# First feed-forward layer of a three-block network: two pairs of column blocks in seven products behind five plain blocks, and the attention's mask added in the down part

## The chip, the cores and the metric

The kernel runs on one core of a Trainium2 chip. The metric is the device time of one execution in microseconds (us). TensorE (PE in the profile, PEld for its weight loads) multiplies, VectorE (DVE) and ScalarE (ACT) work elementwise, GpSimd (POOL) does small work and issues some transfers, SyncE (SP) issues the weight transfers.

## The reference, cut to what matters

The network has 256 tokens of width 1024 and runs a macaron block (feed-forward, attention and pooling mixer, feed-forward, gated projection) and then two more blocks with gated linear attention and retention, each between feed-forward layers. There are six feed-forward layers, all of this form, with an inner width of 2816:

```python
def swiglu(x, w_gate, w_up, w_down):
    return (jax.nn.silu(x @ w_gate) * (x @ w_up)) @ w_down

f = swiglu(rms_norm(h, ffn1_pre_g[i]), ffn1_w_gate[i], ffn1_w_up[i], ffn1_w_down[i])
h = h + 0.5 * rms_norm(f, ffn1_post_g[i])
```

The change touches the first of them, and the bias of the attention that comes behind it (`s = s + bias`, where keys outside a window of 16 columns are left out; the kernel does this with a mask of -1e30 that it adds to the bias).

## The kernel before

All is fp32, and each matmul is done in three: a weight block w is split into a high part (fp32r, made by ScalarE, L1436, tile `split`) and the rest (VectorE, L1876), the tokens likewise (`xh`, `xl`), and PE adds xh·high, xl·high and xh·rest. A weight block holds 4 x 128 rows and 512 columns (1 MB) and is loaded into a tile `whole`; `split` and `whole` are fourteen buffers that a plan hands out (`give_blocks`, by age), and a load or a split waits until PE has passed the block that was last in its buffer.

The gate and up part of a feed-forward layer has eleven column blocks j = 0 to 10 of 256 gate and 256 up columns. A *plain* block is two tiles, ("tile", j, 0) and ("tile", j, 1), one for each half of the 1024 input rows, and each tile is multiplied with both halves of the 256 tokens: 2 x 12 matmuls of 128 x 512. A *pair* of blocks (j, j+1) can instead be done in *seven products* of 12 matmuls each, in the manner of Strassen and Winograd: `b11`, `t1`, `t2`, `b22`, `t3`, `b21`, `t4`. The weights of b11, b22 and b21 are loaded as they are. Those of t1 and t3 are differences of two blocks that stand in memory: SP loads one, and a transfer that GpSimd issues adds the other to it (`pool_sum`, L650; called an addend below). Those of t2 and t4 are sums that VectorE makes (`dve_sum`, L1880). The token side has sums too (`sx`, split into `sh`, `sl`: "token sums" and "blocks"). b11, t2, t3 and t4 gather in PSUM bank 6, t1 with b22 and b21 in bank 7, and the results pass through u1, s5, u2 (ScalarE copies) and the combinations c12, c22, c11 (VectorE, L2157, L2163, L2169). Of the last, c4, there is no copy: ScalarE's gate (L1569) and VectorE's multiplication (L2143) read bank 6 itself.

After a block's silu and multiplication it is transposed by PE (("turn", j), four transposes, L783), split by ScalarE (`th`, L1441) and VectorE (`tl`, L1923), and is the token side of the down part.

What runs when is written out by hand: a list of steps (`LATE_PAIR` for the first layer `f1`, `TWO_PAIRS` for the other five) is walked by PE, ScalarE and VectorE each, and every engine does its part of each step in that order. The splits are run ahead by a few blocks (`ahead`, `behind`, from which buffers are free); in a product step VectorE does its combination, then the splits that are due (`lows()`), then its multiplication. PE's waits in a product are:

```python
def product(g, m):
    if m == "b11":
        if g:
            pe.wait_ge(vec.sem, vec.of("mult", name, grp[g - 1].first, 1))
        pe_product(pe, grp[g].b11, *x_block(0, 0), bank[6], True)
```

so the first product of a second pair waits until VectorE has made the last multiplication of the first pair from bank 6. `turn(7)` of a pair (7, 8) waits in the same way for the multiplication of that pair's c4.

GpSimd walks a list of its own (`pool_program`): two gains and the mask are loaded, then sixteen transfers bring the attention's bias (`pool_bias`), each behind a wait for one of VectorE's splits, with the two addends of f1 among them, and from the ninth on with the additions of the mask (`pool_mask`, L668, sixteen of them) between.

## Time and profile before

| | |
|---|---|
| time, median of 3 runs | 1591.44 us (1590.81 to 1591.67) |
| the profiled execution's own time | 1591.92 us |
| its span | 1590.1 us |
| PE busy | 1580.2 us (99%), 7659 matmuls |
| DVE busy | 1118.8 us (70%) |
| ACT busy | 866.0 us (54%) |
| POOL busy | 105.0 us (7%) |
| gate and up part of f1 on PE, up to the first matmul of the down part | about 6.7 to 132.3 us |

The profile gives for each engine how long it was busy, for a stretch the instructions in order of time (merged where alike), and for an engine what ended its idle time. Starts are from the span's start. The span is 1.8 us shorter than the execution's own time. A matmul of 128 x 512 is listed with 0.39 us and the next one starts 0.227 us after it, since they are pipelined; so PE's progress is read from starts. The same holds in small for DVE and ACT: an operation's listed time is some 0.08 or 0.1 us more than the distance to the next one's start.

### The profile page before, as it was taken

Reading aid. Unit: us, or ns where it says so; the run is one execution under the profiler, and the core shown is the slowest. Engines: PE = TensorE matmul, PEld = TensorE weight load, DVE = VectorE, ACT = ScalarE, POOL = GpSimd, SP = SyncE. Lnnn points to the kernel's source line nnn. Section 1 sums busy time; section 2 is a strip of 40 time slices with the busy share of each in tenths; the row PEclk is TensorE's granted clock in tenths of the full one; section 3 lists DMA queues with packets and bytes.
Section 4 is the critical chain, followed back from the end, with each engine's and each line's share of the span. In section 5 each row is a group of like instructions: output and inputs, shape, how many; then the busy total and the mean of one; then the engine's idle time right before and its main releaser. Section 6 shows DMA issues by size and latency. Waiting matters only on the chain.

```text
span 1590.1 us, 18691 instructions
## 1 busy us (share of the span) xinstructions
PE 1580.2 (99%) x7659; PEld 1317.9 (83%) x7659; DVE 1118.8 (70%) x1081; ACT 866.0 (54%) x907; POOL 105.0 (7%) x126
## 2 busy tenths in 40 slices
PE   9999999999999999999999999999999999999998
PEld 6888897788888888888988888888888998888886
DVE  6785566677875678865668886678856657688964
ACT  7564457556653766642655665366543435456650
POOL 0141000000000000001010000000000131000000
PEclk9999999999999999999999999999999999999999
DMA  8874463467854687562648765578545544587750
GB/s 339 247 237 190 179 245 133 159 252 231 282 181 172 263 280 265 177 240 96 238 159 310 232 225 213 224 229 287 211 185 196 192 172 152 189 292 233 242 212 27
DMA packets 51892, 341.38 MB, mean 215 GB/s; under 512 B 6240, under 2 KB 6624, under 8 KB 13408
## 3 DMA queue, kind: packets, MB, share of 16 engines
q1 hardware_dynamic: 44000, 301.94, 50.7%
q0 software_dynamic: 7584, 38.12, 10.8%
q8 instruction: 61, 1.00, 0.3%
q14 instruction: 23, 0.19, 0.0%
q10 hardware_dynamic: 224, 0.14, 0.0%
HBM read 339.12 MB, written 1.05 MB: 214 GB/s over the span
## 4 chain that ended last, share of the span: by engine, by line
PE 96%; DVE 2%; DMA 1%; ACT 1%; issue 0%; SPq 0%; DVEq 0%; ACTq 0%
PE bank L833 24%; PE bank L846 24%; PE bank L837 21%; PE bank L895 4%; PE bank L897 4%; PE bank L900 4%; PE bank L783 3%; PE bank L850 3%; PE bank L932 1%; PE bank L931 1%; PE bank L929 1%; DVE split L1876 1%; DMA h<-in_x 0%; DMA whole<-in_w_gla 0%; PE bank L1318 0%; PE bank L1108 0%
## 5 line engine op out<-in xcount | busy, mean ns | idle before, releaser
L1876 DVE TENSOR_TENSOR split<-whole,split 128x2048 fp32r<-128x2048 f32 (+2 forms) x329 | 704.4, 2161 | 203.8 <-ACT split L1436 202.1
L1436 ACT ACTIVATE split<-whole 128x2048 fp32r<-128x2048 f32 (+1 forms) x313 | 581.7, 1876 | 265.2 <-DVE whole L1880 38.7
L833 PE MATMUL bank<-split,xh 128*128 128x512 f32 x1052 | 288.1, 396 | 0.0
L846 PE MATMUL bank<-split,xh 128*128 128x512 f32 x1052 | 282.1, 390 | 0.0
L837 PE MATMUL bank<-split,xl 128*128 128x512 f32 x880 | 235.8, 390 | 0.0
L846 PEld LDWEIGHTS bank<-split,xh 128*128 128x128 f32 x1052 | 197.2, 188 | 41.8 <-DVE split L1876 0.4
L833 PEld LDWEIGHTS bank<-split,xh 128*128 128x128 f32 x1052 | 192.9, 188 | 40.7 <-issue 2.8
L837 PEld LDWEIGHTS bank<-split,xl 128*128 128x128 f32 x880 | 165.2, 188 | 35.4
L833 PE MATMUL bank<-split,th 128*128 128x512 f32 x524 | 143.7, 392 | 0.0
L837 PE MATMUL bank<-split,tl 128*128 128x512 f32 x524 | 142.2, 389 | 0.0
L846 PE MATMUL bank<-split,th 128*128 128x512 f32 x524 | 142.1, 389 | 0.0
L837 PEld LDWEIGHTS bank<-split,tl 128*128 128x128 f32 x524 | 98.4, 188 | 20.7
L846 PEld LDWEIGHTS bank<-split,th 128*128 128x128 f32 x524 | 98.4, 188 | 20.6
L833 PEld LDWEIGHTS bank<-split,th 128*128 128x128 f32 x524 | 97.1, 188 | 19.2
L929 PE MATMUL bank<-xh,split 128*128 128x256 f32 x256 | 72.6, 284 | 0.0
L931 PE MATMUL bank<-xl,split 128*128 128x256 f32 x256 | 72.4, 283 | 0.0
L932 PE MATMUL bank<-xh,split 128*128 128x256 f32 x256 | 72.4, 283 | 0.0
L1441 ACT ACTIVATE th<-bank 128x512 fp32r<-128x512 f32 x66 | 39.3, 597 | 29.1 <-PE bank L783 28.1
L1923 DVE TENSOR_TENSOR tl<-bank,th 128x512 fp32r<-128x512 f32 x66 | 45.3, 688 | 13.5 <-ACT th L1441 13.1
L1880 DVE TENSOR_TENSOR whole<-whole 128x2048 f32<-128x2048 f32 x22 | 50.3, 2284 | 0.0
L929 PEld LDWEIGHTS bank<-xh,split 128*128 128x128 f32 x256 | 49.1, 192 | 0.4 <-issue 0.3
L931 PEld LDWEIGHTS bank<-xl,split 128*128 128x128 f32 x256 | 49.1, 192 | 0.0
(312 smaller groups left out, 1727.0 us busy)
## 6 DMA issues: line engine op xcount, KB each, us to landing
whole<-in_w_a_gate_up SPq DMA_DIRECT2D x48, 1024.0 KB, 7.4
whole<-in_w_b_gate_up SPq DMA_DIRECT2D x48, 1024.0 KB, 7.1
whole<-in_w_f_gate_up SPq DMA_DIRECT2D x45, 1024.0 KB, 7.1
whole<-in_w_ret SPq DMA_DIRECT2D x24, 1024.0 KB, 4.9
whole<-in_w_f_down SPq DMA_DIRECT2D x20, 1024.0 KB, 4.9
whole<-in_w_a_down SPq DMA_DIRECT2D x20, 1024.0 KB, 4.9
whole<-in_w_b_down SPq DMA_DIRECT2D x20, 1024.0 KB, 5.1
whole<-in_w_mix SPq DMA_DIRECT2D x16, 1024.0 KB, 4.9
```

Of the source, the lines that this page charges most:

```text
L833: pe.matmul(o[:, :], tokens(0, k), whi[:, k, :], start=start and k == 0, stop=False, skip_group_check=True)
L837: pe.matmul(o[:, :], tokens(1, k), whi[:, k, :], start=False, stop=False, skip_group_check=True)
L846: ins = pe.matmul(o[:, :], tokens(0, k), wlo[:, k, :], start=False, stop=end, skip_group_check=True)
L895: pe.matmul(o[:, :], xh_of(k), whi[:, k, :], start=start and k == 0, stop=False, skip_group_check=True)
L897: pe.matmul(o[:, :], xl_of(k), whi[:, k, :], start=False, stop=False, skip_group_check=True)
L900: ins = pe.matmul(o[:, :], xh_of(k), wlo[:, k, :], start=False, stop=k == 3, skip_group_check=True)
L929: pe.matmul(o, whi[:, k, cols], xh[:, k0 + k, :], start=start and k == 0 and c % 2 == 0, stop=False, skip_group_check=True)
L931: pe.matmul(o, whi[:, k, cols], xl[:, k0 + k, :], start=False, stop=False, skip_group_check=True)
L932: ins = pe.matmul(o, wlo[:, k, cols], xh[:, k0 + k, :], start=False, stop=end, skip_group_check=True)
L1436: act.activation(split[s][:, 0:n], whole[r][:, 0:n], ACT.Copy).then_inc(hi.mark(i), 1)
L1876: dve.tensor_tensor(split[r][:, c0:c1], whole[r][:, c0:c1], split[s][:, c0:c1].bitcast(F32), ALU.subtract).then_inc(lo.mark(*what), 1)
L1880: dve.tensor_tensor(whole[load_to[i]][:, :], whole[load_to[a]][:, :], whole[load_to[b]][:, :], ALU.add).then_inc(vec.mark("sum", i), 1)
```

## The change

`LATE_PAIRS` takes the place of `LATE_PAIR`: blocks 5 and 6, which were plain, become a pair of seven products too. The order is blocks 0 to 3, tile (4, 0), the first product of pair (5, 6), tile (4, 1), and then the 14 products with the plain blocks 9 and 10 among them. GpSimd gets two more addends, and all sixteen bias transfers come first; the mask is added behind them, each two additions behind a split of one of the first blocks of the down part.

```diff
-LATE_PAIR = (
+LATE_PAIRS = (
...
-    ("tile", 4, 0), ("tile", 4, 1), ("turn", 3),
-    ("product", 0, "b11"), ("tile", 5, 0),
-    ("product", 0, "t1"), ("tile", 5, 1), ("turn", 4),
-    ("product", 0, "t2"), ("tile", 6, 0),
-    ("product", 0, "b22"), ("tile", 6, 1), ("turn", 5),
-    ("product", 0, "t3"), ("tile", 9, 0), ("turn", 6),
-    ("product", 0, "b21"), ("tile", 9, 1), ("turn", 8),
-    ("product", 0, "t4"), ("tile", 10, 0), ("tile", 10, 1), ("turn", 9), ("turn", 7))
+    ("tile", 4, 0), ("turn", 3),
+    ("product", 0, "b11"), ("tile", 4, 1),
+    ("product", 0, "t1"), ("product", 0, "t2"), ("tile", 9, 0), ("turn", 4),
+    ("product", 0, "b22"), ("product", 0, "t3"), ("tile", 9, 1),
+    ("product", 0, "b21"), ("product", 0, "t4"), ("turn", 6),
+    ("product", 1, "b11"), ("turn", 5), ("tile", 10, 0),
+    ("product", 1, "t1"), ("product", 1, "t2"), ("tile", 10, 1),
+    ("product", 1, "b22"), ("product", 1, "t3"), ("turn", 9),
+    ("product", 1, "b21"), ("product", 1, "t4"), ("turn", 8), ("turn", 7))
...
-LATE, TWO = Order(LATE_PAIR, 7), Order(TWO_PAIRS, 3, 7)
+LATE, TWO = Order(LATE_PAIRS, 5, 7), Order(TWO_PAIRS, 3, 7)
...
             for n in range(8):
-                if n == 2:
+                if n == 1:
                     pool_sum(pool, "t1", group["f1", 0].t1)
-                if n == 7:
+                if n == 5:
                     pool_sum(pool, "t3", group["f1", 0].t3)
                 pool.wait_ge(lo.sem, lo.of(6 + n))
                 pool_bias(0, n)
             for n in range(8):
+                if n == 3:
+                    pool_sum(pool, "t1", group["f1", 1].t1)
+                if n == 7:
+                    pool_sum(pool, "t3", group["f1", 1].t3)
                 pool.wait_ge(lo.sem, lo.of(14 + n))
                 pool_bias(1, n)
-                if n == 0:
-                    pool.wait_ge(bias_in[0].sem, bias_in[0].of(7))
-                pool_mask(0, n)
-            for hd in range(8):
-                pool.wait_ge(lo.sem, lo.of(22 + hd))
-                if hd == 0:
-                    pool.wait_ge(bias_in[1].sem, bias_in[1].of(7))
-                pool_mask(1, hd)
+            for t in range(2):
+                pool.wait_ge(bias_in[t].sem, bias_in[t].of(7))
+                for hd in range(8):
+                    pool.wait_ge(lo.sem, lo.of(at["f1d"][t] + hd // 2))
+                    pool_mask(t, hd)
```

The first place, PE, where the last product of a pair (t4, into bank 6) ends. Before, in the order of the program: t4 of the only pair, then block 10 in banks 0 and 1 (the first of its two tiles is shown).

```order
L783 MATMUL bank5<-ident,xn 128x128 x4
L895 MATMUL bank6<-split2,xh 128x512 x4
L897 MATMUL bank6<-split2,xl 128x512 x4
L900 MATMUL bank6<-split0,xh 128x512 x4
L833 MATMUL bank0<-split6,xh 128x512 x4
L837 MATMUL bank0<-split6,xl 128x512 x4
L846 MATMUL bank0<-split9,xh 128x512 x4
```

After, the last product of the first pair, one turn, and the first product of the second pair, again into bank 6 (lines stand two lower, L895 is L897):

```order
L897 MATMUL bank6<-split6,xh 128x512 x4
L899 MATMUL bank6<-split6,xl 128x512 x4
L902 MATMUL bank6<-split0,xh 128x512 x4
L785 MATMUL bank5<-ident,xn 128x128 x4
L897 MATMUL bank6<-split2,xh 128x512 x4
L899 MATMUL bank6<-split2,xl 128x512 x4
L902 MATMUL bank6<-split5,xh 128x512 x4
L785 MATMUL bank4<-ident,xn 128x128 x4
```

What moved: between the last product of a pair and the next user of bank 6 there stand four transposes now, where two tiles and the turn of block 9 stood.

The second place, VectorE (DVE), where the weights of t1 and t2 are made. Before, for the only pair: turn 3's `tl`, the rest of tile (5, 0), the sum for t2, the rest of t1, the rest of tile (5, 1), the sum for t4, the rest of t2.

```order
L1923 TENSOR_TENSOR tl0<-bank5,th0 128x512
L1876 TENSOR_TENSOR split0<-whole0,split11 128x2048
L1880 TENSOR_TENSOR whole6<-whole9,whole5 128x2048
L1876 TENSOR_TENSOR split5<-whole5,split4 128x2048
L1876 TENSOR_TENSOR split2<-whole2,split10 128x2048
L1880 TENSOR_TENSOR whole0<-whole3,whole6 128x2048
L1876 TENSOR_TENSOR split6<-whole6,split7 128x2048
```

After, for the second pair: turn 6's `tl`, the rest of tile (10, 0), turn 5's `tl`, the sum for t2, the rest of t1, the sum for t4, the rest of t2, of tile (10, 1), b22, t3 and b21.

```order
L1925 TENSOR_TENSOR tl0<-bank5,th0 128x512
L1878 TENSOR_TENSOR split1<-whole1,split3 128x2048
L1925 TENSOR_TENSOR tl0<-bank4,th0 128x512
L1882 TENSOR_TENSOR whole0<-whole10,whole4 128x2048
L1878 TENSOR_TENSOR split4<-whole4,split8 128x2048
L1882 TENSOR_TENSOR whole2<-whole11,whole0 128x2048
L1878 TENSOR_TENSOR split0<-whole0,split6 128x2048
L1878 TENSOR_TENSOR split9<-whole9,split5 128x2048
L1878 TENSOR_TENSOR split10<-whole10,split1 128x2048
L1878 TENSOR_TENSOR split7<-whole7,split3 128x2048
L1878 TENSOR_TENSOR split11<-whole11,split4 128x2048
```

What moved: eight weight-sized operations stand behind one turn's `tl` now, and there is one plain tile on PE between the turn and t1.

The third place is the end of the gate and up part. PE before, the end of tile (10, 1), turn 9, turn 7 (which needs c4, whose product stands 48 matmuls earlier) and the down part's first block:

```order
L833 MATMUL bank1<-split7,xh 128x512 x4
L837 MATMUL bank1<-split7,xl 128x512 x4
L846 MATMUL bank1<-split4,xh 128x512 x4
L783 MATMUL bank4<-ident,hh0 128x128 x4
L783 MATMUL bank5<-ident,xn 128x128 x4
L833 MATMUL bank6<-split3,th0 128x512 x2
```

After, t4 of the second pair, turn 8, turn 7 and the down part's first block:

```order
L897 MATMUL bank6<-split0,xh 128x512 x4
L899 MATMUL bank6<-split0,xl 128x512 x4
L902 MATMUL bank6<-split2,xh 128x512 x4
L785 MATMUL bank4<-ident,xn 128x128 x4
L785 MATMUL bank5<-ident,xn 128x128 x4
L835 MATMUL bank6<-split5,th0 128x512 x2
```

What moved: the turn that needs c4 stands one turn behind the product that makes it.

VectorE there, before: turn 8's `tl`, the rests of the down part's first three blocks with the multiplication from bank 6 among them, block 10's two multiplications and the `tl` of turn 9.

```order
L1923 TENSOR_TENSOR tl0<-bank5,th0 128x512
L1876 TENSOR_TENSOR split8<-whole8,split3 128x1024
L2143 SCALAR_TENSOR_TENSOR xn<-bank6,st,xn 128x256
L1876 TENSOR_TENSOR split10<-whole10,split1 128x1024
L1876 TENSOR_TENSOR split11<-whole11,split0 128x2048
L2143 SCALAR_TENSOR_TENSOR hh0<-bank0,st,sg0 128x256
L2143 SCALAR_TENSOR_TENSOR hh0<-bank1,st,sg0 128x256
L1923 TENSOR_TENSOR tl0<-bank4,th0 128x512
```

After: the combination c11, the rests of the down part's second and third block, the multiplications from u1 and from bank 6, the `tl` of turns 8 and 7.

```order
L2171 TENSOR_TENSOR xn<-bank7,xn 128x512
L1878 TENSOR_TENSOR split6<-whole6,split1 128x1024
L1878 TENSOR_TENSOR split9<-whole9,split3 128x2048
L2145 SCALAR_TENSOR_TENSOR xn<-xn,st 128x256
L2145 SCALAR_TENSOR_TENSOR xn<-bank6,st,xn 128x256
L1925 TENSOR_TENSOR tl0<-bank4,th0 128x512
L1925 TENSOR_TENSOR tl0<-bank5,th0 128x512
```

What moved: two rests (1.5 of the full size) and the multiplication from u1 stand between c11 and the multiplication from bank 6, and turn 7 is next on PE.

## Rows read from the trace of the kernel before

**Rows 1.** The page: busy time of each engine, then PE's granted clock in 40 slices.
```profile
PE 1580.2 (99%) x7659; PEld 1317.9 (83%) x7659; DVE 1118.8 (70%) x1081; ACT 866.0 (54%) x907; POOL 105.0 (7%) x126
...
PEclk9999999999999999999999999999999999999999
```
**Rows 2.** PE's waits over the whole span: us in total, times, longest.
```profile
PE bank L783 <- DMA h<-in_x: 1.3, 1, 1.3
...
PE bank L1228 <- DVE xn L2371: 0.3, 1, 0.3
```
**Rows 3.** PE in order of time, f1: start us, us, line, xcount.
```profile
66.55 0.60 PE L783 MATMUL bank<-ident,hh 128*128 128x128 f32 x4
66.91 1.17 PE L895 MATMUL bank<-split,xh 128*128 128x512 f32 x4
...
69.74 1.07 PE L833 MATMUL bank<-split,xh 128*128 128x512 f32 x4
...
75.18 1.07 PE L895 MATMUL bank<-split,sh 128*128 128x512 f32 x4
...
77.90 1.07 PE L833 MATMUL bank<-split,xh 128*128 128x512 f32 x4
...
120.64 1.07 PE L833 MATMUL bank<-split,xh 128*128 128x512 f32 x4
...
131.52 0.60 PE L783 MATMUL bank<-ident,hh 128*128 128x128 f32 x4
131.96 0.60 PE L783 MATMUL bank<-ident,xn 128*128 128x128 f32 x4
```
**Rows 4.** ACT in order of time, f1: a turn's high part, and c4's gate.
```profile
67.19 0.60 ACT L1441 ACTIVATE th<-bank 128x512 fp32r<-128x512 f32 x1
...
120.83 0.47 ACT L1569 ACTIVATE xn<-bank,st 128x256 f32<-128x256 f32 x1 [1.21 <-PE bank L900]
```
**Rows 5.** DVE in order of time, f1.
```profile
67.82 0.69 DVE L1923 TENSOR_TENSOR tl<-bank,th 128x512 fp32r<-128x512 f32 x1
68.42 2.28 DVE L1876 TENSOR_TENSOR split<-whole,split 128x2048 fp32r<-128x2048 f32 x1
70.62 2.29 DVE L1880 TENSOR_TENSOR whole<-whole 128x2048 f32<-128x2048 f32 x1
...
83.83 0.87 DVE L2143 SCALAR_TENSOR_TENSOR hh<-bank,st,sg 128x256 f32<-128x256 f32 x2
...
119.54 1.21 DVE L1876 TENSOR_TENSOR split<-whole,split 128x1024 fp32r<-128x1024 f32 x1
121.34 0.48 DVE L2143 SCALAR_TENSOR_TENSOR xn<-bank,st,xn 128x256 f32<-128x256 f32 x1 [0.59 <-ACT xn L1569]
```
**Rows 6.** PE in order of time in f2, turn 3 behind the second pair's first product.
```profile
427.97 0.60 PE L783 MATMUL bank<-ident,xn 128*128 128x128 f32 x4
```
**Rows 7.** ACT there: u1's copy, then the turn's high part.
```profile
430.77 0.58 ACT L1585 ACTIVATE xn<-bank 128x512 f32<-128x512 f32 x1
431.25 0.59 ACT L1441 ACTIVATE th<-bank 128x512 fp32r<-128x512 f32 x1
```
**Rows 8.** DVE there: the rest of t1, then the turn's low part.
```profile
428.83 2.29 DVE L1876 TENSOR_TENSOR split<-whole,split 128x2048 fp32r<-128x2048 f32 x1
431.87 0.69 DVE L1923 TENSOR_TENSOR tl<-bank,th 128x512 fp32r<-128x512 f32 x1 [0.76 <-ACT th L1441]
```
**Rows 9.** PE in order of time, where it waited for DVE.
```profile
770.73 0.48 PE L1205 MATMUL bank<-xn 32*128 32x256 f32 x2 [0.40 <-DVE xn L2324]
```
**Rows 10.** DVE there: what PE waited for.
```profile
770.26 0.41 DVE L2324 COPY xn<-bank 64x256 f32<-64x256 f32 x1
```
**Rows 11.** DVE from 20 to 130 us by line and form: xcount | busy us, mean ns | idle.
```profile
L1876 DVE TENSOR_TENSOR split<-whole,split 128x2048 fp32r<-128x2048 f32 x24 | 56.5, 2373 | 6.5 <-ACT split L1436 6.5
```
**Rows 12.** DVE in order of time, a split while POOL adds the mask.
```profile
99.18 3.34 DVE L1876 TENSOR_TENSOR split<-whole,split 128x2048 fp32r<-128x2048 f32 x1
```
**Rows 13.** POOL there.
```profile
99.61 0.74 POOL L668 TENSOR_TENSOR bias<-bias,mask 128x256 f32<-128x256 f32 x1
```
**Rows 14.** All 22 addends (L650): time to landing.
```profile
DMA to landing us min/median/max: 7.9/10.5/13.4
```

## The prediction, made before the changed kernel had run

> **What bounds the kernel now.** First the page: PE is busy 99% of the span and its granted clock stands at the top in all 40 slices, which is the 2.4 GHz level, while DVE has 70% and ACT 54% [rows 1]. Then PE's waits: there are four rows in the whole span, and together they are 3.2 us; the longest is for the first input, at the very start, and none is in the stretch that the change touches [rows 2]. So the time is the number of matmuls by 0.227 us. What shortens PE's list shortens the time one for one, and what makes PE wait adds to it one for one. Last, PE in order of time through f1's gate and up part: groups of four matmuls that follow at 0.907 us, which gives 2.72 us for a product (from 75.18 to 77.90), 5.44 us for a tile (69.74 to 75.18), and for a product behind a turn 2.83 us (66.91 to 69.74), since the array starts again; a turn takes 0.36 us (66.55 to 66.91), and 0.44 where a second turn follows it [rows 3].
>
> **What the change takes away.** Four plain tiles (96 matmuls) become seven products (84). Turns stay eleven. That is 12 x 0.227 = 2.72 us less on PE. It is the whole gain; I know of no other, since PE waits for nothing that the change could end.
>
> **What it adds on DVE.** A product's block lasts PE 2.72 us, a tile's 5.44. Three extra blocks are to be split, and two extra sums made, and each is 2.20 us of DVE (from 68.42 to 70.62) [rows 5]; a multiplication is 0.40, a `tl` or a combination 0.60 (67.82 to 68.42), half a block 1.13. PE reads a block's rest only in the last third of a product, 1.81 us after its start. I laid the new order of DVE beside PE's, with these steps, and looked for each rest that is late.
>
> The anchor is a turn on PE. Its `th` starts 0.64 us later (66.55, 67.19) and its `tl` 1.27 us later (67.82) [rows 3 to 5].
>
> *Pair (5, 6).* Turn 3 starts at 61.11 now, 5.44 us before its old 66.55. Behind its `tl` DVE has a rest, sum, rest, sum, rest, two multiplications, and the rest of tile (9, 0): 1.27 + 0.60 + 5 x 2.20 + 0.80 + 2.28 = 15.95 us after the turn. PE wants it at 0.36 + 2.83 + 5.44 + 2.72 + 2.72 + 1.81 = 15.88. To the 0.07 comes DVE's signal to PE, 0.06 us (770.67 to 770.73) [rows 9, 10], and the restart, 0.11: about **0.2 us**. The rest of t2 ahead of it is in time by 0.2.
>
> *Between the pairs.* The first product of pair (7, 8) goes into bank 6, which ACT's gate and DVE's multiplication of c4 still read. In the kernel before, t4 ended at 120.64, the gate ran from 120.83 to 121.30, the multiplication from 121.34 to 121.82: 1.18 us [rows 3 to 5], hidden by block 10. Now turn 6 (0.36) is all that covers it. 1.18 + 0.06 - 0.36 = **0.9 us** of wait. DVE is free for it: c11, a rest and a multiplication before it (3.2 us) start 0.2 us behind b21's end, 2.52 us before t4's.
>
> *Pair (7, 8), the sums.* Here turn 5 stands behind the new pair's b11, and u1's copy on ACT waits for that turn and stands ahead of its `th`: 0.48 us, as in f2 (430.77, 431.25) [rows 7]. So `tl` starts 0.64 + 0.48 + 0.63 = 1.75 us after the turn. In f2 the same place lets PE through: turn 3 is at 427.97, and the first sum and the rest of t1 stand ahead of `tl` there (428.83 is the rest, `tl` 431.87) [rows 6, 8]. In the new f1 both stand behind it. The rest of t2 is ready at 1.75 + 0.60 + 3 x 2.20 + 2.28 + 0.06 = 11.29 us after the turn; PE wants it at 0.36 + 5.58 (a tile behind a turn) + 2.72 + 1.81 = 10.47. Late by 0.82, and with the restart **0.9 us**.
>
> *The end of pair (7, 8).* From that `tl` on DVE has no pause. To the end of the multiplication of c4 it holds 0.60 + 8 x 2.20 + 2 x 0.40 + 0.60 + 2.20 + 0.40 + 0.60 + 1.13 + 0.40 + 2 x 0.60 + 1.13 + 2.20 + 0.40 + 0.48 = 29.7 us, so turn 7 may start 1.75 + 29.7 + 0.06 = 31.5 us after turn 5. PE's own way there is 0.36 + 5.58 + 2 x 2.72 + 5.44 + 2 x 2.72 + 0.36 + 2.83 + 2.72 + 0.44 = 28.6, with the 0.9 above 29.5. PE waits **2.0 us** more. Were DVE free, it would still be 1.18 + 0.06 - 0.44 = 0.8, by the same c4 chain. The reason for the other 1.2 is that two rests of the down part (3.3 us) stand ahead of the multiplication.
>
> **The mask.** Its sixteen additions leave the gate and up part, where they cost PE nothing (it did not wait) and DVE something: of its 24 full splits there the mean is 2.37 us and not 2.28 [rows 11], 2.2 us of excess in all, and half of that is one split of 3.34 beside POOL's 99.61 [rows 12, 13]. Now they start when the first down block's rest is made, about 5 us before turn 7 and inside DVE's unbroken chain; five or so fall there. Bounds for one: nothing, and 1.06 (the excess of the longest). I take the mean, 2.2 / 16 = 0.14, since it is over many: **0.7 us** for five, 0 to 5.3 as bounds. The others run in the down part, where DVE has idle time and PE's blocks last 2.72 or 5.44 us; their cost there is nothing, and the attention reads the bias some 100 us later.
>
> The Trainium skill (SBUF — State Buffer, the part on the two sides of SBUF) says that DVE, with two inputs in SBUF, and GpSimd hold their shared port pair exclusively and that the other blocks fully for the whole instruction. The 3.34 agrees that they hinder each other; the mean of all splits is far below what the rule would make of it. By the rule, five additions would hold DVE 0.74 us each, and the sum would be 3.0 us higher.
>
> **DMA.** One load more and two addends more. An addend lands 7.9 to 13.4 us after its issue, 10.5 in the middle, in 22 of them [rows 14]. The first of pair (7, 8) is issued behind a rest of tile (9, 1), about 84.5, and wanted on ACT at 98.7, with 1.7 us of play behind that until u1's copy: 16 us. The second is issued behind tile (10, 0)'s rest at about 102.5 and wanted at about 115: 13 us. Those of pair (5, 6) have more. So they cost nothing by the middle, and the last almost touches the longest seen. SP's loads are gated by PE's passes as before; the tightest is tile (10, 0)'s, which is issued at 83.9 beside an addend and wanted by about 95.7, ahead of c4's gate on ACT.
>
> **Sum.** -2.72 + 0.2 + 0.9 + 0.9 + 2.0 + 0.7 = +2.0 us. The profiled execution's own time of 1591.92 (span 1590.1) would be 1593.9; it lies 0.5 over the median of 1591.44, and on that the forecast is **1593.4 us**. This kernel's measurement can tell about 0.2% (3.2 us) from no change: faster is under 1588.3, slower over 1594.6. The gain by itself, 0.17%, is under that.
>
> **The rivals.**
> *Only the bank waits remain.* My steps for DVE are too long, or ACT is earlier, so that its chain of 30 us is hidden; then 0.9 and 0.8 stay: -2.72 + 1.7 = -1.0, **1590.4**. For it: the chain misses by 0.8 in 11 and by 2 in 31, a few per cent. Against: the steps of 2.20 are the same in all rows.
> *The full gain.* -2.7, **1588.7**. It needs the wait for bank 6 to be hidden, and nothing stands between t4 and b11 but a turn.
> *Slower, by a late addend.* GpSimd's list puts pair (7, 8)'s addends behind bias transfers, and these behind DVE's rests, which are themselves late. It decides when the second one takes over 13 us from issue to landing or the first over 16; then all of DVE's chain slides. With 16 and 19 us (more than any seen, as it would be with four addends in the stretch) it is 3 us: **1596.4**. For: 13.4 was seen, and DMA has more to carry. Against: the second ones are issued when few loads run.
> *Slower, by the mask.* Six additions each hold DVE for 0.74 us (the duration of POOL's row) right ahead of turn 7: 4.4 in place of 0.7, **1597.1**. It decides only if they fall between c22 and the multiplication of c4; for it speaks the split of 3.34, against it the mean of all. This is also what the port rule above leads to.
>
> **How the numbers follow.** Forecast (1592.4 to 1594.8) 0.55; only the bank waits 0.22; full gain 0.03; late addend 0.13; mask 0.07. The range takes in the bank waits and the late addend: 1590.2 to 1596.6; what is left out is the full gain, the mask and tails. Faster by over 0.2%: 0.03. Slower: addend and mask, 0.20, and 0.05 of the forecast's tail, 0.25. Within: 0.72.
>
> **What would show it.** In the new trace PE's waits should have new rows: one for b11 of pair (7, 8) near 97.9, 0.9 us, ended by DVE's multiplication from bank 6; one for t2's last group near 112, 0.8; one for turn 7 near 131, 2 to 3, ended by the same multiplication. The down part's first block should start at about 133.5, against 132.31 at the old place. DVE should run without idle from turn 5's `tl` (about 103.3) to there. If PE shows no wait for b11, my reading of bank 6 is wrong. If DVE idles in that chain for ACT, and ACT for a landing, it is the addend. If DVE's operations there are longer than 2.28, it is the mask. The forecast is wrong in sign if the down part starts before 132.3.

## The result, and the profile after

The changed kernel takes 1596.55 us (median of 7 runs, 1595.5 to 1597.65) where the kernel before, beside it on the same chip, takes 1591.44 (7 runs). The ratio is 1.003, 95% interval 1.0019 to 1.0042: 5.1 us, or 0.3%, slower. The forecast was 1593.4 us, range 1590.2 to 1596.6. So the time lies inside the range by 0.05 us only, 3.2 us above the forecast, and what was named the likeliest (within 0.2%) did not come true: "slower by over 0.2%", which had 0.25, did. The profiled execution took 1595.5 us, its span is 1593.7: 3.6 more than the span before.

First the page of the changed kernel, beside [rows 1]. TensorE has 12 matmuls fewer, as forecast, and is busy 1.6 us less; VectorE has 12 us more.

```profile
PE 1578.6 (99%) x7647; PEld 1316.0 (83%) x7647; DVE 1130.8 (71%) x1089; ACT 872.5 (55%) x913; POOL 104.0 (7%) x128
```

Then PE's waits in the whole span (us in total, times, longest). [Rows 2] had four. Three in the stretch of the change are new: those for DVE at L785 (a turn), L902 (third group of a product) and L897 (first group). A fourth new one, 0.6 us for ACT at L862, is at the start of the program, where every profiled execution waits a little differently; the two at L1205 and L1228 are gone.

```profile
PE bank L785 <- DVE xn L2145: 3.7, 1, 3.7
...
PE bank L902 <- DVE split L1878: 0.7, 1, 0.7
PE bank L897 <- DVE xn L2145: 0.6, 1, 0.6
```

PE in order of time at these three places: b11 of pair (7, 8) behind turn 6, the last group of t2, and turn 7 behind turn 8 with the down part's first groups (start us, us, line, xcount, in brackets the idle time before it). A group starts late by its start less that of the turn ahead and 0.36 (0.44 between two turns): 0.88 at b11 and 3.87 at turn 7. In t2 the step between two groups is 1.81 in place of 0.91, and the next is 1.04: 1.03 in all.

```profile
97.25 0.60 PE L785 MATMUL bank<-ident,xn 128*128 128x128 f32 x4
98.49 0.50 PE L897 MATMUL bank<-split,xh 128*128 128x512 f32 x1 [0.65 <-DVE xn L2145]
...
110.90 1.07 PE L899 MATMUL bank<-split,sl 128*128 128x512 f32 x4
112.71 0.50 PE L902 MATMUL bank<-split,sh 128*128 128x512 f32 x1 [0.74 <-DVE split L1878]
...
130.56 0.60 PE L785 MATMUL bank<-ident,xn 128*128 128x128 f32 x4
134.87 1.11 PE L785 MATMUL bank<-ident,xn 128*128 128x128 f32 x4 [3.71 <-DVE xn L2145]
135.63 1.20 PE L835 MATMUL bank<-split,th 128*128 128x512 f32 x2
136.63 1.05 PE L839 MATMUL bank<-split,tl 128*128 128x512 f32 x2
137.48 0.74 PE L848 MATMUL bank<-split,th 128*128 128x512 f32 x2
138.06 0.62 PE L835 MATMUL bank<-split,th 128*128 128x512 f32 x2
```

The last lines show something besides waits: behind the wait of 3.7 us a group of two matmuls takes 1.0 and 0.85 us, and only later 0.46 (in e2, below, 0.54 and then 0.47 from the start). The table of stretches says why (stretch: length, busy us and instructions of PE, PEld, DVE, ACT and POOL, then PE's granted clock, DMA share, GB/s): the clock fell near the end of the wait (0.94 in the mean over it), is at 0.50 of full behind it, the 1.2 GHz level, and back at 1.00 after 138 us.

```profile
130.50:134.80 4.30, 0.65 (x5) 0.35 (x3) 4.30 (x5) 2.80 (x4) 3.38 (x2) 0.94 0.00 0
134.80:136.00 1.20, 1.14 (x5) 1.14 (x6) 0.60 (x2) 0.00 (x0) 1.20 (x3) 0.50 0.00 0
136.00:137.50 1.50, 1.50 (x5) 1.11 (x5) 0.86 (x2) 0.60 (x1) 0.37 (x1) 0.50 0.04 11
138.00:142.00 4.00, 4.00 (x19) 3.29 (x19) 1.53 (x1) 0.00 (x0) 2.39 (x4) 1.00 0.32 88
```

DVE in order of time, from turn 5's `tl` to the multiplication of c4 for which turn 7 waits. It has two pauses, both for ACT: 0.69 us for a high part and 0.42 us for the gate of block 10 (L1571), which ACT reached at 122.19 without a stop since 115.80. And it has one instruction that is twice as long as its like, the multiplication of u1 (0.94 us; the one at 128.47 takes 0.48).

```profile
103.16 0.69 DVE L1925 TENSOR_TENSOR tl<-bank,th 128x512 fp32r<-128x512 f32 x1 [1.76 <-ACT th L1443]
...
117.75 2.29 DVE L1878 TENSOR_TENSOR split<-whole,split 128x2048 fp32r<-128x2048 f32 x1 [0.69 <-ACT split L1438]
...
122.76 0.88 DVE L2145 SCALAR_TENSOR_TENSOR hh<-bank,st,sg 128x256 f32<-128x256 f32 x2 [0.42 <-ACT sg L1571]
...
128.47 0.48 DVE L2145 SCALAR_TENSOR_TENSOR xn<-xn,st 128x256 f32<-128x256 f32 x1
...
130.07 3.48 DVE L1878 TENSOR_TENSOR split<-whole,split 128x1024 fp32r<-128x1024 f32 x2
133.47 0.94 DVE L2145 SCALAR_TENSOR_TENSOR xn<-xn,st 128x256 f32<-128x256 f32 x1
134.34 0.47 DVE L2145 SCALAR_TENSOR_TENSOR xn<-bank,st,xn 128x256 f32<-128x256 f32 x1
```

ACT, which was waited for, stood still itself, for a load and then for the second adding transfer of the pair; and GpSimd had issued that one at 106.20 only, 3.83 us after it was free to, because the block that it adds to had not been loaded. SP had issued that load at 92.0 and it took 13.9 us; in e4 (below) SP issued the same load at 91.9 and it took 8.8, so it was the transfer that was slow and not its issue. The adding transfer landed at 115.8. ACT's two rows:

```profile
110.27 3.72 ACT L1438 ACTIVATE split<-whole 128x2048 fp32r<-128x2048 f32 x2 [2.27 <-DMA whole<-in_w_f_gate_up]
115.80 1.92 ACT L1438 ACTIVATE split<-whole 128x2048 fp32r<-128x2048 f32 x1 [1.81 <-DMA whole<-in_w_f_gate_up]
```

GpSimd in order of time:

```profile
106.20 0.93 POOL L651 DMA_DIRECT2D whole<-in_w_f_gate_up  x1 [3.83 <-DMA whole<-in_w_f_gate_up]
```

The DMA engines were full there (a share near 1 leaves none of the 16 idle). The same stretch, 84 to 116 us, first of the kernel before (DMA share 0.80), then of the changed one (1.02):

```profile
84.00:116.00 32.00, 32.00 (x146) 26.45 (x145) 26.30 (x22) 20.52 (x20) 16.84 (x17) 1.00 0.80 257
```
```profile
84.00:116.00 32.00, 30.61 (x138) 24.82 (x137) 26.73 (x21) 16.48 (x17) 5.56 (x8) 1.00 1.02 288
```

### The profile page after: what moved, and what is told of

It is laid out like the page before. It is cut to its first block, busy times and chain, and to the rows that moved or that the text cites. A ratio compares the mean times of both kernels' runs of the same rounds, so it can differ in the third digit from the quotient of the medians.

```text
span 1593.7 us, 18696 instructions
## 1 busy us (share of the span) xinstructions
PE 1578.6 (99%) x7647; PEld 1316.0 (83%) x7647; DVE 1130.8 (71%) x1089; ACT 872.5 (55%) x913; POOL 104.0 (7%) x128
## 4 chain that ended last, share of the span: by engine, by line
PE 96%; DMA 2%; DVE 1%; issue 0%; ACT 0%; SPq 0%; DVEq 0%; ACTq 0%
PE bank L835 24%; PE bank L848 24%; PE bank L839 21%; PE bank L897 4%; PE bank L899 4%; PE bank L902 4%; PE bank L785 3%; PE bank L852 3%; PE bank L931 2%; PE bank L933 2%; PE bank L934 2%; DMA whole<-in_w_f_gate_up 1%; DMA h<-in_x 0%; PE bank L1320 0%; DVE split L1878 0%; PE bank L1110 0%
## 5 line engine op out<-in xcount | busy, mean ns | idle before, releaser
L1438 ACT ACTIVATE split<-whole 128x2048 fp32r<-128x2048 f32 (+1 forms) x316 | 587.9, 1877 | 256.8 <-DVE whole L1882 42.9
L835 PE MATMUL bank<-split,xh 128*128 128x512 f32 x1020 | 279.7, 396 | 0.0
L848 PE MATMUL bank<-split,xh 128*128 128x512 f32 x1020 | 273.6, 390 | 0.0
L839 PE MATMUL bank<-split,xl 128*128 128x512 f32 x848 | 227.2, 390 | 0.0
L848 PEld LDWEIGHTS bank<-split,xh 128*128 128x128 f32 x1020 | 191.1, 188 | 40.9 <-DVE split L1878 0.6
L835 PEld LDWEIGHTS bank<-split,xh 128*128 128x128 f32 x1020 | 186.9, 188 | 39.3 <-issue 2.8
L839 PEld LDWEIGHTS bank<-split,xl 128*128 128x128 f32 x848 | 159.2, 188 | 34.1
L835 PE MATMUL bank<-split,th 128*128 128x512 f32 x524 | 144.2, 393 | 0.0
L835 PEld LDWEIGHTS bank<-split,th 128*128 128x128 f32 x524 | 97.4, 188 | 19.2
L1882 DVE TENSOR_TENSOR whole<-whole 128x2048 f32<-128x2048 f32 x24 | 54.8, 2283 | 0.0
L897 PE MATMUL bank<-split,sh 128*128 128x512 f32 x192 | 52.5, 395 | 0.0
L902 PE MATMUL bank<-split,sh 128*128 128x512 f32 x192 | 51.5, 390 | 0.7 <-DVE split L1878 0.7
```

The source lines that it names most:

```text
L835: pe.matmul(o[:, :], tokens(0, k), whi[:, k, :], start=start and k == 0, stop=False, skip_group_check=True)
L839: pe.matmul(o[:, :], tokens(1, k), whi[:, k, :], start=False, stop=False, skip_group_check=True)
L848: ins = pe.matmul(o[:, :], tokens(0, k), wlo[:, k, :], start=False, stop=end, skip_group_check=True)
L897: pe.matmul(o[:, :], xh_of(k), whi[:, k, :], start=start and k == 0, stop=False, skip_group_check=True)
L902: ins = pe.matmul(o[:, :], xh_of(k), wlo[:, k, :], start=False, stop=k == 3, skip_group_check=True)
L1438: act.activation(split[s][:, 0:n], whole[r][:, 0:n], ACT.Copy).then_inc(hi.mark(i), 1)
```

## The experiments

The first question was what the 3.7 us at turn 7 are made of. My theory: VectorE's chain (2.0 us, as forecast), made longer by the late adding transfer and by the mask, and then the clock's fall as a consequence of the wait. The rivals: the mask's additions alone; a clock that falls for reasons of its own; DMA work that has nothing to do with it. The second question was whether the waits are separate costs or one. Each of the twelve kernels was timed beside the kernel before, 5 to 11 executions of each, on four chips. There the kernel before has medians of 1591.36 to 1591.68 us, so a difference between two rows of the table can be off by some tenths of a us. The waits are those of the one profiled execution.

| run | median us | ratio to before, 95% | wait at turn 7, us |
|---|---|---|---|
| changed kernel | 1596.55 | 1.0019 to 1.0042 | 3.7 |
| e1_mask_only | 1591.65 | 0.9990 to 1.0007 | none |
| e2_hold | 1591.76 | 0.9993 to 1.0011 | 0.7 |
| e3_fill | 1595.42 | 1.0014 to 1.0036 | 0.5 behind the filling |
| e4_bias_late | 1592.58 | 1.0003 to 1.0021 | 1.8 |
| e5_between | 1598.36 | 1.0027 to 1.0055 | 2.3 |
| e6_tail | 1599.53 | 1.0037 to 1.0062 | none; 5.5 ahead of b22 |
| e7_no_mask | 1595.88 | 1.0016 to 1.0036 | 3.4 |
| e8_hold_late | 1591.61 | 0.9993 to 1.0010 | 0.6 |
| e9_defer | 1596.27 | 1.0019 to 1.0042 | 3.9 |
| e10_defer_late | 1591.46 | 0.9990 to 1.0008 | 1.8 |
| e11_between_late | 1591.18 | 0.9991 to 1.0009 | 1.9 |
| e12_between_hold_late | 1589.62 | 0.9978 to 0.9996 | 0.6 |

**The mask by itself** (e1). The kernel before, with this part of the change alone:

```diff
                 pool.wait_ge(lo.sem, lo.of(14 + n))
                 pool_bias(1, n)
-                if n == 0:
-                    pool.wait_ge(bias_in[0].sem, bias_in[0].of(7))
-                pool_mask(0, n)
-            for hd in range(8):
-                ...
-                pool_mask(1, hd)
+            for t in range(2):
+                pool.wait_ge(bias_in[t].sem, bias_in[t].of(7))
+                for hd in range(8):
+                    pool.wait_ge(lo.sem, lo.of(at["f1d"][t] + hd // 2))
+                    pool_mask(t, hd)
```

> The kernel before, with only the mask's additions moved into the down part (its order of blocks and its eight products for the first feed-forward layer stay). If the mask's additions matter only because they fall on VectorE's full stretch of the changed order, this run is within 0.7 us of the kernel before (1591.4 us), since VectorE has idle time in the down part of the kernel before. Rival: the additions themselves cost, wherever the order stands, about 0.5 to 2 us, and then this run is at 1592 to 1593.5 us and a good part of the +5.1 us of the changed kernel is theirs.

It stays at the time of before: 1591.65 us. The additions cost nothing that shows where VectorE has room.

**The down part's share of the chain** (e2). In the changed kernel, on ScalarE and on VectorE alike:

```diff
 elif step == "product":
-    act_high(act, ahead(spot[(name, *what)], 1))
+    last = name == "f1" and tuple(what) in ((1, "b21"), (1, "t4"))
+    if not last:
+        act_high(act, ahead(spot[(name, *what)], 1))
     product(*what)
```

> The changed kernel, with the high parts on ScalarE and the remainders on VectorE of the block b21 and the sum t4 of pair (7,8) put behind the multiplication of c4 (about 9 us of VectorE's work leave the chain ahead of it). Theory: turn 7 waits 3.7 us because VectorE is late with c4's multiplication, and the granted clock falls behind that wait. Then the wait at turn 7 falls to under 1 us, the clock stays at 1.0 behind it, and the run is 3.5 to 5 us below the changed kernel, at 1591.5 to 1593 us. Rival one: what is held back is only late at its next reader (the down part's first blocks), and the wait comes back there: within 1 us of the changed kernel. Rival two: the clock falls for another reason than the wait; then about 1.4 us of the loss stays, at about 1594 us.

1591.76 us, 4.8 less than the changed kernel. PE in order of time at turns 8 and 7: the wait is 0.73 and the clock stays at 1.00 (the down part's second group on L835 starts at 134.38, 1.88 us behind turn 7, against 3.19); nothing comes back in the down part.

```profile
131.17 0.60 PE L785 MATMUL bank<-ident,xn 128*128 128x128 f32 x4
132.50 0.66 PE L785 MATMUL bank<-ident,xn 128*128 128x128 f32 x4 [0.73 <-DVE xn L2147]
132.91 0.70 PE L835 MATMUL bank<-split,th 128*128 128x512 f32 x2
```

So the loss at turn 7 but for the last 0.9 us, clock and all, hangs on the work that stands ahead of c4's multiplication. That was the theory; both rivals fall for this run. The edit takes work from ScalarE as well as from VectorE, and no run takes it from one alone; in the changed kernel ScalarE's gate of c4 ended at 132.8 us and VectorE came to the multiplication at 134.34, so VectorE was the later one.

**The clock** (e3). The changed kernel with fifteen matmuls ahead of turn 7 whose result nothing reads:

```diff
+            for _ in range(15):
+                pe.matmul(b[:, :], xh[:, 0, 0:P], xh[:, 0:2, :].rearrange("p k n -> p (k n)"), start=True, stop=True)
             pe.wait_ge(vec.sem, ready)
```

> The changed kernel with 15 matmuls of 128x512 more (no result of theirs is used), placed into the wait ahead of turn 7, so that TensorE is busy there while VectorE comes to c4's multiplication. 15 x 0.216 us are 3.2 us, less than the wait of 3.7 us. Theory: the granted clock of 0.5 behind the wait (134.3 to 137.7 us) follows from TensorE standing still; then it stays at 1.0 here and the run is about 1.4 us below the changed kernel, at 1595.2 us. Rival: the clock falls for another reason (the stretch's own work); then nothing is gained, 1596.5 us or some tenths more, and the granted clock is still 0.5 at 134 to 138 us.

1595.42 us, 1.1 less than the changed kernel. PE with the filling, then the granted clock in that stretch:

```profile
133.65 0.60 PE L785 MATMUL bank<-ident,xn 128*128 128x128 f32 x4
134.00 3.70 PE L791 MATMUL bank<-xh 128*128 128x512 f32 x15
138.15 0.66 PE L795 MATMUL bank<-ident,xn 128*128 128x128 f32 x4 [0.45 <-DVE xn L2159]
```
```profile
134.00:138.00 4.00, 3.70 (x18) 2.72 (x16) 4.00 (x4) 2.58 (x4) 3.31 (x2) 1.00 0.00 0
```

Turn 7 is as late as before the edit (4.5 us behind turn 8, against 4.3), and the clock stays at 1.00. The other executions say the same: the mean granted clock of one is 0.999 or 1.000 in six of the seven of e3, and 0.997 or 0.998 in all seven of the changed kernel. So the fall follows from TensorE standing still. It costs 1.3 us by the trace (from turn 7 to the down part's second group on L835: 3.19 us in the changed kernel, 1.88 in e2); the 1.1 us between the medians fit, but are within what these few executions scatter. The profiled execution of e3 is its longest, 1597.97 us: the clock fell in it at the start of the program, which with longer waits there puts the rows above about 3 us later than their like (see the last section).

**The adding transfers** (e4). GpSimd's list in the changed kernel, the four adding transfers first:

```diff
-            for n in range(8):
-                if n == 1:
-                    pool_sum(pool, "t1", group["f1", 0].t1)
-                ...
+            pool.wait_ge(lo.sem, lo.of(6))
+            for m, g in (("t1", 0), ("t3", 0), ("t1", 1), ("t3", 1)):
+                pool_sum(pool, m, getattr(group["f1", g], m))
+            for t in range(2):
+                for n in range(8):
+                    pool.wait_ge(lo.sem, lo.of(28 + (8 * t + n) // 4))
+                    pool_bias(t, n)
```

> The changed kernel with the bias transfers on GpSimd's queue all behind the four adding transfers of the two pairs, so that fewer bytes compete between 84 and 116 us. Theory: the second adding transfer of pair (7,8) lands late (115.8 us) because the DMA engines are fully busy and its own block's load is late with it; without the bias it lands 1.5 to 3 us earlier, ScalarE's and VectorE's wait for it at 112 to 118 us goes by about 1.4 us, and turn 7's wait falls from 3.7 to about 2.3 us: about 1.4 us less, 1595.1 us. Rival: the weights alone fill the DMA engines; the landing stays within 0.5 us of 115.8 us and the run within 0.4 us of the changed kernel.

1592.58 us, 4.0 less than the changed kernel (3.3 by the spans of the two profiled executions), where I had expected 1.4. The second adding transfer is issued at 101.03 and lands 9.1 us later, at 110.2, 5.6 earlier than in the changed kernel; DVE has no pause from 103.16 on. The edit does two things to the engines' load ahead of that: it takes the bias away, and it issues the pair's first adding transfer at 79.98 in place of 84.19; which of them made the loads faster was not separated. The same stretch as above, DMA share 0.85:

```profile
84.00:116.00 32.00, 30.61 (x137) 24.75 (x137) 26.68 (x21) 19.78 (x19) 0.86 (x1) 1.00 0.85 274
```

PE at turns 8 and 7:

```profile
130.59 0.60 PE L778 MATMUL bank<-ident,xn 128*128 128x128 f32 x4
132.95 0.66 PE L778 MATMUL bank<-ident,xn 128*128 128x128 f32 x4 [1.76 <-DVE xn L2138]
133.36 0.70 PE L828 MATMUL bank<-split,th 128*128 128x512 f32 x2
```

Turn 7 starts 1.92 us late and not 3.87. The 1.95 are the late transfer and the mask together (its additions, too, stand behind the bias here and no longer fall beside the chain). DVE's rows divide them: from the `tl` at 103.16, which stands at the same time in both, it reaches block 10's multiplication 1.38 us earlier (121.38 for 122.76) and gains 0.54 more behind it. And behind the wait of 1.8 us the clock was at 1.00, which gives the other 1.3. The mask and the clock are what my expectation left out. The clock did not stay up each time, it seems: four of e4's eleven executions have a mean granted clock of 0.997 or 0.998, and they are the four longest, 1594.2 to 1595.2 us, with the others at 1592.1 to 1592.7.

**The mask in its place** (e7). The changed kernel with additions of one element; the rest of the mask is left out, and the attention's result changes by it:

```diff
-                pool.tensor_tensor(bias[:, t, hd, :, :], bias[:, t, hd, :, :], ...
+                pool.tensor_tensor(bias[:, t, hd, 0, 0:1], bias[:, t, hd, 0, 0:1], mask[:, 0:1], ALU.add)
```

> The changed kernel with each of the mask's additions cut down to one element, so that the bias goes on almost without the mask: the 16 additions of 0.6 to 0.8 us on GpSimd are left out, and the attention's result changes by it. Theory: the additions run while VectorE finishes c3's and c4's multiplications and stretch the one of u1 by 0.47 us; without them c4's multiplication ends 0.3 to 0.5 us earlier, the wait at turn 7 is 3.2 to 3.4 us, and the run is 0.3 to 1 us below the changed kernel (more if the shorter wait keeps the clock up). Rival: the additions hold VectorE back for about their whole length (16 x 0.7 us, of which 5 to 6 fall ahead of turn 7): 2 to 3.5 us less.

1595.88 us, 0.7 less. DVE: u1's multiplication is short again.

```profile
133.96 0.47 DVE L2144 SCALAR_TENSOR_TENSOR xn<-xn,st 128x256 f32<-128x256 f32 x1
```

So the mask costs 0.47 us on the chain, in one instruction, and the rival of 2 to 3.5 us falls. The difference of the medians is no sharper than that. The wait at turn 7 is 3.4 us here, since the adding transfer was issued later still, at 107.75 (DVE stands 1.7 us for ACT at 118.31). In the profiled execution the clock did not fall behind it; six of the eight executions have a mean granted clock of 0.997 or 0.998, and they are the six longest.

**Separate waits or one?** (e5, e6, e9.) Two runs move a tile to where PE waits, the third takes away the pause of VectorE ahead of turn 5's remainder.

```diff
-    ("product", 1, "b11"), ("turn", 5), ("tile", 10, 0),
+    ("tile", 10, 0), ("product", 1, "b11"), ("turn", 5),
```


> The changed kernel with the tile (10,0) moved ahead of the product b11 of pair (7,8), behind turn 6, so that 5.4 us of matmuls that need nothing of VectorE stand where b11 waits for c4's multiplication of the pair before (wait 0.65 us, start of the next group 0.89 us later than without it). Theory one: that wait goes and the later ones grow by about as much, since VectorE has no idle time from 103 us on and turn 7 waits for the end of its chain: the run is within 0.7 us of the changed kernel (1595.9 to 1597.2 us). Rival: each wait costs by itself; then 0.9 us are gained, at 1595.6 us, and turn 7 still waits 3.7 us.

```diff
-    ("product", 1, "t1"), ("product", 1, "t2"), ("tile", 10, 1),
+    ("product", 1, "t1"), ("product", 1, "t2"),
...
-    ("product", 1, "b21"), ("product", 1, "t4"), ("turn", 8), ("turn", 7))
+    ("product", 1, "b21"), ("product", 1, "t4"), ("turn", 8), ("tile", 10, 1), ("turn", 7))
```


> The changed kernel with the tile (10,1), 5.4 us of matmuls that need nothing of VectorE, moved from behind t2 of pair (7,8) to the place between turn 8 and turn 7. Theory: VectorE's chain is the bound of this stretch, so the wait of 3.7 us at turn 7 comes back as waits at b22, t3, b21 and t4, which now stand 5.4 us earlier and need remainders of the same chain; but TensorE works right up to turn 7 or waits less there at a time, so that the granted clock stays at 1.0: about 1.4 us gained at most, 1595 to 1597 us. Rival: the remainders of those blocks are ready early enough, and the tile covers the wait: 3.7 us plus the clock's 1.4 us gained, 1591.5 us.

Both came out slower than both theories, 1598.36 and 1599.53 us. In e5 the wait at b11 is gone, but t2 waits; in e6 turn 7 does not wait, but b22 does, and b11 waits 3.1 us and not 0.6. PE of e5, then of e6:

```profile
112.29 2.08 PE L897 MATMUL bank<-split,sh 128*128 128x512 f32 x4 [3.13 <-ACT xn L1587]
```
```profile
121.13 1.22 PE L897 MATMUL bank<-split,sh 128*128 128x512 f32 x2 [5.50 <-ACT xn L1592]
```

Both wait for ACT's copy that empties a bank, and that copy is queued behind a high part for which ACT waits for a transfer. In e5 it is a plain load, issued at 94.6, for which ACT stood 4.37 us until 109.84; in e6 it is the adding transfer. ACT of e6:

```profile
116.88 3.71 ACT L1438 ACTIVATE split<-whole 128x2048 fp32r<-128x2048 f32 x2 [8.12 <-DMA whole<-in_w_f_gate_up]
120.50 0.58 ACT L1592 ACTIVATE xn<-bank 128x512 f32<-128x512 f32 x1
```

So a product that is put earlier runs into a late landing (116.9 us in e6). In both the clock fell as well (0.81 in the mean of 100 to 118 us in e5, 0.72 in that of 118 to 130 in e6). e5's row above shows it: its four matmuls took 1.87 us to the next group, where 0.91 is the rule.

The third, with one instruction moved:

```diff
 elif step == "turn":
-    turn(*what)
+    if name != "f1" or what[0] != 5:
+        turn(*what)
...
+if name == "f1" and (step, *what) == ("tile", 10, 0):
+    turn(5)
```


> The changed kernel with one instruction of VectorE moved: turn 5's remainder, for which VectorE stands still from 101.4 to 103.2 us, comes behind the next block's sum and remainder. Theory: VectorE gains 1.8 us there and the wait at t2's last group (1.0 us) goes; but turn 7 is then held by the second adding transfer (landed 115.8 us) and what ScalarE and VectorE do after it, which does not move, so that turn 7's wait grows by the same 1.0 us, from 3.7 to 4.7 us: the run is within 0.7 us of the changed kernel (1596.0 to 1597.2 us). Rival: VectorE's work alone sets turn 7; then both waits shrink, by 1.8 us in all, with or without the clock's 1.4 us: 1593.3 to 1594.8 us.

1596.27 us, the time of the changed kernel. The wait at t2 is gone, but what is gained there is lost again: ACT still stands for the transfer, which lands at 116.3, and DVE for ACT. That is the theory's end, though not its place. The wait at turn 7 was to grow to 4.7 us and is 3.9; the 1.0 us came back ahead of turn 8, in short waits at tile (10, 1), b21 and t4 (the PE row), so that turn 8 is at 130.88 us, no earlier than the 130.56 of the changed kernel (the program's start is 0.3 us longer in e9). The changed kernel's wait at t2 is no cost of its own while the transfer is late.

```profile
116.32 1.92 ACT L1438 ACTIVATE split<-whole 128x2048 fp32r<-128x2048 f32 x1 [1.80 <-DMA whole<-in_w_f_gate_up]
```
```profile
128.01 1.20 PE L897 MATMUL bank<-split,xh 128*128 128x512 f32 x4 [0.17 <-DVE xn L2165]
```

**Two edits at a time** (e8, e10, e11). The edits are those above: hold and late bias; the moved remainder and late bias; the tile ahead of b11 and late bias.

> The changed kernel with both edits of earlier runs: ScalarE's and VectorE's work for b21 and t4 of the down part behind c4's multiplication, and the bias transfers behind the four adding ones. Each alone left a wait at turn 7 of 0.7 and 1.8 us, with the clock at 1.0. Theory: the two act on the same chain, so no wait is left at turn 7, and what stays of the change's loss are the waits of b11 (0.9 us) and of t2's last group (1.0 us): a sum of -2.7 + 0.2 + 0.9 + 1.0 = -0.6 us against the kernel before, about 1591 us. Rival: with the wait at turn 7 gone the late down-part work or the late bias becomes the wait instead (first blocks of the down part, or the attention's first scores): 1592 us or more.

> The same move of turn 5's remainder, and the bias transfers behind the four adding ones. The latter alone left 1.8 us at turn 7 (there VectorE had no idle time from 103.2 us on) and 1.0 us at t2's last group. Theory: with the transfers early, VectorE's own work is what is left, and 1.8 us less of idle time take the wait at t2's last group and most of the one at turn 7; only b11's 0.9 us stays: -2.7 + 0.2 + 0.9 + 0 to 0.5 = -1.6 to -1.1 us against the kernel before, 1589.8 to 1590.3 us. Rival: the adding transfer, landing at 110.2 us, is the next bound and gives the 1.8 us back at 111 to 118 us: 1592.5 us, as without the move.

> The order of the earlier run with tile (10,0) ahead of b11 of pair (7,8), which was 1.8 us slower than the changed kernel with a wait of 3.1 us ahead of t2's products, and now with the bias transfers behind the four adding ones. Theory: that wait came from ScalarE, which stood still for the adding transfer (landed 115.1 us) and its own block's load with the copy that frees the bank queued behind; the transfers landing some 5 us earlier take it away, and b11's wait is covered by the tile: 1591 to 1592.5 us, 6 to 7 us less than that run. Rival: the products simply stand too early for VectorE's and ScalarE's chain; then 2 us or more of that wait stay, at 1594 us or more.

e11 bears out the theory on e5 that the transfers, and not the place of the product, made it slow: 1591.18 us, 7.2 less than e5, and neither b11 nor t2 waits. e8 and e10 gave 1591.61 and 1591.46 where I had expected about 1591 and 1590. The step that failed is the same in both: a wait at turn 7 stays. In e8 it is 0.6 us. In e10, and in e11 too, it is 1.8 and 1.9 us as in e4, though VectorE was relieved of 1.8 us of idle time; that relief took away only the wait at t2. DVE of e10 shows why: it waits for PE now, at the end of b22, and from there on has no pause.

```profile
121.46 0.69 DVE L2152 TENSOR_TENSOR xn<-bank,xn 128x512 f32<-128x512 f32 x1 [0.68 <-PE bank L895]
...
127.99 3.42 DVE L1871 TENSOR_TENSOR split<-whole,split 128x1024 fp32r<-128x1024 f32 x2
131.33 0.47 DVE L2138 SCALAR_TENSOR_TENSOR xn<-xn,st 128x256 f32<-128x256 f32 x1
131.73 0.47 DVE L2138 SCALAR_TENSOR_TENSOR xn<-bank,st,xn 128x256 f32<-128x256 f32 x1
```

PE, at turns 8 and 7 of e10:

```profile
129.90 0.60 PE L778 MATMUL bank<-ident,xn 128*128 128x128 f32 x4
132.26 0.66 PE L778 MATMUL bank<-ident,xn 128*128 128x128 f32 x4 [1.76 <-DVE xn L2138]
```

From b22's end DVE has 132.20 - 121.46 = 10.7 us of work to the end of c4's multiplication. PE could start turn 7 at 129.90 + 0.44 = 130.34, 8.9 us behind the same point. The difference is 1.9 us, a bound by itself, and neither relief ahead of b22 (e10, e11) moved it.

**Three edits together** (e12): hold, late bias, and the tile ahead of b11.

> Three edits of earlier runs together: tile (10,0) ahead of b11 of pair (7,8), the bias transfers behind the four adding ones, and the high parts and remainders for b21 and t4 of the down part behind c4's multiplication. Theory: what was left at turn 7 in the last two runs (1.8 and 1.9 us, with the transfers early and VectorE's idle time gone) is local: VectorE has 10.6 us of work between the end of b22 and c4's multiplication, where TensorE has 8.9 us, so that only work taken out of exactly this stretch helps. 3.4 us of remainders are taken out; then at most 0.6 us are waited at turn 7, b11 and t2 don't wait, and the run is 1.2 to 2 us below the kernel before, at 1589.5 to 1590.3 us. Rival: the work held back is missed at the down part's first blocks once everything ahead of them is earlier, or the wait returns as one for ScalarE; then the run is within 0.7 us of the kernel before.

1589.62 us, ratio 0.9987 (0.9978 to 0.9996): 2.1 us below the kernel before beside it (1591.68), 6.9 below the changed one, and faster than both; its longest execution, 1590.25, is shorter than the shortest of the kernel before, 1591.06. PE's waits no longer have b11 or t2 among them, and turn 7's is 0.6:

```profile
PE bank L778 <- DVE xn L2140: 0.6, 1, 0.6
```

With the wait it starts 0.8 us late. That is the chain of c4's gate and multiplication, which the prediction had priced at 1.18 + 0.06 - 0.44 = 0.8 for a free VectorE.

## Why the prediction was right where it was, and wrong where it was

Taken off the profiled executions of before and after, place by place, up to the down part's first groups (the last row lies behind them):

| step | forecast | measured |
|---|---|---|
| 12 matmuls less | -2.72 | -2.72 |
| remainder of tile (9, 0), pair (5, 6) | +0.2 | +0.22 |
| b11 of pair (7, 8) waits for bank 6 | +0.9 | +0.89 |
| remainder of t2, pair (7, 8) | +0.9 | +1.03 |
| turn 7 behind VectorE's chain | +2.0 | +1.92 (as e4 shows it alone) |
| mask beside the chain | +0.7 | +0.47 |
| late adding transfer, with the late load ahead of it | 0 | +1.48 |
| clock behind turn 7's wait | not thought of | +1.3 to 1.4 |
| start of the program | 0 | -0.5 |
| two later waits of before that are gone | 0 | -0.8 |

Turn 7 of after is 3.87 late; less the 1.92 and the 0.47, 1.48 are left for the transfer (DVE's rows against e4's give 1.38, and 0.54 for the mask). The column adds up to +3.3, the spans differ by 3.6. By the medians the difference is 5.1, interval 3.0 to 6.7; the profiled execution of after was the shortest of its runs, and what the others lost beyond the table stays open.

*In the range by luck.* The sum was +2.0 us, and +5.1 were measured (+3.6 in the profiled executions). The range reached that far for one rival only, an adding transfer that costs 3 us. What filled it was 1.5 us of that kind and 1.3 us of a fallen clock, which was not thought of.

*Right.* All three new waits stand at the places and with the releasers that were named (98.5 for 97.9 us, 112.7 for 112, 134.9 for 131 plus 2 to 3), and four terms of the sum are within 0.15 us. They were sums of steps of 2.20 and 0.60 us over up to 31 us; those steps hold. (The sentence that the kernel's time is the number of matmuls by 0.227 us does not: 7659 of them would be 1739 us. That step is one of 512 columns, and many have fewer. Nothing in the sum hangs on it.) The rival "only the bank waits" is refuted by its own condition: VectorE's chain was not shorter. The 0.8 us that were to stay with a free VectorE were measured in e12.

*Mis-sized: the DMA.* The step said that the adding transfers "cost nothing by the middle, and the last almost touches the longest seen". The time from issue to landing was in bounds, 9.6 us for the second one and 13.9 for the first (limits 13 and 16). What failed is the point of issue: it was put behind tile (10, 0)'s remainder, at 102.5, and GpSimd was free at 102.4, but the block that it adds to was itself loaded late, and the issue slid to 106.2. The loads were judged by when SP issues them, and that was as before; they were not judged by the share of the engines. The five loads of 84 to 116 us took 14.5 us in the middle to land, against 5.2 for the three of the kernel before. The rival "slower, by a late addend" had the right effect and end (DVE idle for ACT, ACT for a landing) and gave 1596.4 us, but its size came from a longer transfer, which did not happen; and its 3 us are 1.5 in the trace.

*Missed: the clock.* A wait of more than 2 us at one place was forecast, and what TensorE's clock does behind one was not asked. It is the largest cost that the prediction did not ask about, 1.3 us.

*The mask.* The mean of 0.14 us for each of five additions was the wrong picture, if not far off in sum: one instruction was stretched by 0.47, the others by nothing that shows. GpSimd was the one to pay. The four additions between 131 and 136.5 us, by line (duration min/median/max in ns, first and last start):

```profile
L669 POOL TENSOR_TENSOR bias<-bias,mask x4: 724/814/2703, 131.4 to 135.6; 128x256 f32<-128x256 f32 x4
```

The first, started at 131.43 while DVE made a remainder (the 3.48 us of two in the row at 130.07), took 2.70 us, that is, until behind the remainder's end at 133.55, and DVE's next instruction, u1's multiplication, then stood for it. The Trainium skill (SBUF — State Buffer, Who interferes with whom) says that the order of issue decides who blocks, and that a VectorE instruction with at most one input in SBUF, outside its 2-port modes, does not contend with GpSimd. The trace agrees with both: the addition that came second waited, and c4's multiplication, which reads the bank, took 0.47 us beside the next addition, where u1's, which reads SBUF alone, had taken 0.94. So here VectorE was held once in the four additions that began before the end of c4's multiplication, and for part of one; the 3.0 us more that the prediction derived from the lock did not come.

*Not explained.* Two short waits of before far behind the change (L1205 and L1228, 0.4 and 0.3 us, [rows 2, 9]) are missing in the changed kernel and in e12, which gives 0.7 to 0.8 us; no run asked why. In e1 the first of them is there.

## What to carry to other kernels

A change that takes work off the bounding engine and gives it to the next one has to be summed on the second engine stretch by stretch, each from the last point where it waits for the first; here relief ahead of such a point did not shorten the wait behind it (e10, e11). For transfers, ask not only how long one takes but when its issue may happen and how full the engines are by then, with the loads that it waits for. And work for a later stage that an engine's list puts ahead of the last release of this one should be moved behind it: here that, with an earlier adding transfer and one moved tile, made 6.9 us of difference and a loss into a gain.

## What the runs showed of the hardware that I had not expected

- TensorE's granted clock went to 0.50 (1.2 GHz) behind waits of 3.7 us (changed kernel), 3.9 (e9), 3.1 (e5) and 5.5 (e6), in e5 also behind one of 2.3, and in e3 at the start of the program, where a wait of 1.70 us (the row below) follows one of 1.46 at 7.06: 0.73 over 10 to 12 us and 0.50 over 12 to 14. It stayed at 1.00 in the traces behind waits of 1.8 (e4, e10), 1.9 (e11), and also behind 3.1 (e6, at 101 us) and 3.4 (e7). So the length of a wait alone does not decide it between 1.7 and 3.4 us, and for the same kernel some executions fall and some do not, as the mean clocks of e4 and e7 show. What decides it was not settled. The Trainium skill (TensorE: Matmul & The Clock Gate, Why this matters for your kernels) warns of idle gaps between stretches of matmuls for this reason. The trace agrees in kind, with the waits listed here.

```profile
10.69 0.94 PE L785 MATMUL bank<-ident,h 128*128 128x128 f32 x4 [1.70 <-DMA h<-in_x]
```

- The packets of an adding transfer took about twice the time of the engines that those of a plain load of the same bytes took. Where no bias runs beside them (e4, 84 to 116 us) the two kinds of queue divide as follows (packets, MB, share of 16 engines): 54.6% of 32 us for 6.93 MB is 2.5 us for a MB, 29.8% for 1.84 MB is 5.2.

```profile
q1 hardware_dynamic: 1052, 6.93, 54.6%
q0 software_dynamic: 256, 1.84, 29.8%
```
